# Output projection of the last two token tiles in two contraction halves, with block 4's weights loaded between them

## The reference, cut to what matters

```python
a = _rmsnorm(h, norm_mix)
proj = a @ w_in
...
h = h + jnp.concatenate([pool_out, ssd_out], axis=-1) @ w_out
h = h + _hier_moe(_rmsnorm(h, norm_ffn), router_grp_w, router_grp_b, router_exp_w, ...)
gate = jax.nn.sigmoid((_rmsnorm(h, norm_ple) @ ple_gate_w + ple_gate_b).astype(jnp.float32))
h = h + (gate * (p @ ple_proj_w).astype(jnp.float32)).astype(h.dtype)
```

## Time and profile before

| | us |
|---|---|
| median of 3 runs | 543.52 |
| the three runs | 545.23, 543.52, 539.91 |
| the profiled execution, whole | 540.01 |
| its span, first to last instruction | 538.2 |
| TensorE busy with matmuls | 503.0 (93% of the span) |
| VectorE busy | 214.2 (40%) |
| ScalarE busy | 154.3 (29%) |
| GpSimd busy | 111.6 (21%) |
| expert weights, one matrix | 1024 KB, 32 each of gate, up and down |

### The profile page before, as it was taken

One profiled execution on the slowest core, in us unless ns is written; L12 is line 12 of the kernel. 1 busy time (PEld: TensorE's weight loads), 2 busy tenths in 40 slices (PEclk: granted clock), 3 DMA queues, 4 the chain that ended last, 5 costly groups with the idle time before them and its releaser, 6 DMA issues.

```text
span 538.2 us, 7829 instructions
## 1 busy us (share of the span) xinstructions
PE 503.0 (93%) x3122; PEld 308.0 (57%) x3122; DVE 214.2 (40%) x509; ACT 154.3 (29%) x318; POOL 111.6 (21%) x169
## 2 busy tenths in 40 slices
PE   5999999999999999799999999988888989999993
PEld 4888886888545555455555555544444543444453
DVE  2187696523034556662222222212111111579344
ACT  1436263112524121112222222221121224454123
POOL 0300058994201002101111211110111112031001
PEclk9999999999999999899999999998988999999997
DMA  8993000604469905999999999999999996941012
GB/s 308 399 327 110 1 1 7 229 1 95 156 242 395 381 5 181 404 406 411 416 414 417 412 419 414 414 418 414 417 416 416 416 411 252 373 170 40 2 40 79
DMA packets 41577, 145.71 MB, mean 271 GB/s; under 512 B 14620, under 2 KB 15260, under 8 KB 32420
## 3 DMA queue, kind: packets, MB, share of 16 engines
q1 hardware_dynamic: 33956, 131.77, 62.3%
q0 software_dynamic: 5152, 8.71, 4.4%
q10 hardware_dynamic: 2432, 4.71, 2.3%
HBM read 141.24 MB, written 15.24 MB: 291 GB/s over the span
## 4 chain that ended last, share of the span: by engine, by line
PE 71%; DMA 12%; SPq 8%; DVE 6%; ACT 1%; issue 1%; POOLq 0%; ACTq 0%; POOL 0%; DVEq 0%
PE PS L1047 13%; PE PS L833 10%; PE PS L1161 10%; PE PS L639 10%; DMA mem<-in_exp_w_up 9%; PE PS L1068 7%; PE PS L610 6%; PE PS L599 5%; SPq L493 3%; SPq L497 2%; SPq L491 2%; DVE mem L1720 1%; PE PS L897 1%; DMA mem<-choice_rows 1%; DMA mem<-in_w_a 1%
## 5 line engine op out<-in xcount | busy, mean ns | idle before, releaser
L1047 PE MATMUL PS<-mem 128*64 128x256 f32 x512 | 122.1, 393 | 13.2 <-DMA mem<-in_exp_w_up 13.0
L1048 PE MATMUL PS<-mem 128*64 128x256 f32 x512 | 122.2, 394 | 0.0
L1047 PEld LDWEIGHTS PS<-mem 128*64 128x64 f32 x512 | 69.6, 141 | 49.5 <-DMA mem<-in_exp_w_up 10.6
L639 PE MATMUL PS<-mem 128*128 128x260 f32 x320 | 73.3, 386 | 0.0
L1048 PEld LDWEIGHTS PS<-mem 128*64 128x64 f32 x512 | 69.7, 141 | 0.0
L639 PEld LDWEIGHTS PS<-mem 128*128 128x128 f32 x320 | 60.0, 190 | 10.4 <-issue 1.5
L2021 DVE TENSOR_TENSOR mem<-PS,mem 64x256 f32<-64x256 f32 x32 | 13.7, 427 | 128.6 <-ACT mem L1364 128.4
L1068 PE MATMUL PS<-mem 128*64 128x512 f32 x256 | 62.0, 605 | 1.1 <-ACT mem L1370 0.7
L833 PE MATMUL PS<-mem 128*128 128x512 f32 x128 | 56.6, 596 | 0.0
L1161 PE MATMUL PS<-mem 128*128 128x512 f32 (+1 forms) x144 | 56.0, 547 | 0.0
L1364 ACT ACTIVATE mem<-PS 64x256 f32<-64x256 f32 x32 | 12.0, 375 | 113.3 <-PE PS L1048 113.3
(11 more groups left out here) (290 smaller groups left out, 550.4 us busy)
## 6 DMA issues: line engine op xcount, KB each, us to landing
mem<-in_exp_w_down SPq DMA_DIRECT2D x32, 1024.0 KB, 23.8
mem<-in_exp_w_gate SPq DMA_DIRECT2D x32, 1024.0 KB, 21.5
mem<-in_exp_w_up SPq DMA_DIRECT2D x32, 1024.0 KB, 23.5
mem<-in_w_out SPq DMA_DIRECT2D x2, 2048.0 KB, 7.3
mem<-in_ple_gate_w SPq DMA_DIRECT2D x2, 2048.0 KB, 16.6
mem<-choice_rows SPq DMA_DIRECT2D x4, 1024.0 KB, 13.4
mem<-in_x_prompt SPq DMA_DIRECT2D x4, 512.0 KB, 14.5
mem<-in_w_v SPq DMA_DIRECT2D x1, 2048.0 KB, 24.9
```

Of the source, the lines that this page charges most:

```text
L639: ins = pe.matmul(PS[b + h][:, 0:HALF], w[:, k, :], aT[:, k, h * HALF:(h + 1) * HALF], start=(k == 0), stop=(k == KT - 1))
L1047: pe.matmul(PS[0][0:S, 0:FF], rows_k, gu[slot][:, k, :], start=(k == 0), stop=(k == KT - 1))
L1048: ins = pe.matmul(PS[1][S:2 * S, 0:FF], rows_k, gu[slot][:, KT + k, :], start=(k == 0), stop=(k == KT - 1))
```

## The change

Places 3 and 4 run row groups 0 to 3 of both column halves first (`outproj_part(3, 0, 4)`, `outproj_part(4, 0, 4)`), then row groups 4 to 7. After the first half of place 4 the third count of the semaphore `s_gn_done`, now named `s_gn_part_done`, is given. SyncE waits for it and loads block 4's gate and up weights and the down weights of block 6; after all ten signals of `s_outp_done` it loads block 5's gate, up and down weights. On VectorE both residual additions of place 3 come after `place(1)`, and that of place 4's first column half after `take_h(3, 1)`.

```diff
+            sp.wait_ge(s_gn_part_done, 3)
+            load_gate_up(gu_slot(4), bass.ds(4, 1))
+            load_down(dn_slot(6), bass.ds(6, 1))
             sp.wait_ge(s_outp_done, 2 * NT)
-            for b in (4, 5):
-                load_gate_up(gu_slot(b), bass.ds(b, 1))
-            for b in (5, 6):
-                load_down(dn_slot(b), bass.ds(b, 1))
+            load_gate_up(gu_slot(5), bass.ds(5, 1))
+            load_down(dn_slot(5), bass.ds(5, 1))
...
             h_rows(1, 0)
             h_rows(1, 1)
             pe.wait_ge(s_outp_out, 4)
-            out_half(3, 0, 0, KT)
+            outproj_part(3, 0, 4)
             route(1)
             h_rows(2, 0)
             h_rows(2, 1)
             count(0)
-            out_half(3, 1, 0, KT)
+            pe.wait_ge(s_outp_out, 6)
+            outproj_part(4, 0, 4).then_inc(s_gn_part_done, 1)
             route(2)
             count(1)
-            pe.wait_ge(s_outp_out, 6)
-            out_half(4, 0, 0, KT)
+            out_half(3, 0, 4, KT)
+            out_half(3, 1, 4, KT)
+            out_half(4, 0, 4, 6)
             h_rows(3, 0)
             h_rows(3, 1)
             count(2)
-            out_half(4, 1, 0, 2)
+            out_half(4, 0, 6, KT)
             route(3)
+            out_half(4, 1, 4, 5)
             h_rows(4, 0)
             first_pair_slots()
-            out_half(4, 1, 2, 6)
+            out_half(4, 1, 5, 7)
             count(3)
-            out_half(4, 1, 6, KT)
+            out_half(4, 1, 7, KT)
...
             choose(0)
-            residual(3, 0)
             take_logits(1)
...
             place(0)
-            residual(3, 1)
             take_logits(2)
             choose(2)
             rank(1)
             place(1)
-            residual(4, 0)
+            residual(3, 0)
+            residual(3, 1)
             take_h(3, 0)
             take_h(3, 1)
+            residual(4, 0)
             rank(2)
             place(2)
             take_logits(3)
```

More of the change, by code:

```diff
@@ L419, in build @@
         s_gated = sem("s_gated")
-        s_gn_done = sem("s_gn_done")
+        s_gn_part_done = sem("s_gn_part_done")
         s_gn_ln = sem("s_gn_ln")
@@ L860, in _ @@
                                     start=True, stop=True)
-                ins.then_inc(s_gn_done, 1)
+                ins.then_inc(s_gn_part_done, 1)
             pe.wait_ge(s_inproj_out, len(COLS) - NA)
@@ L1315, in _ @@
             for g in range(2):
-                act.wait_ge(s_gn_done, g + 1)
+                act.wait_ge(s_gn_part_done, g + 1)
                 for h in range(2):
```

## The result

| | before | changed |
|---|---|---|
| median of 22 runs each, us | 542.4 | 543.89 |
| lowest and highest, us | 539.26, 545.23 | 541.98, 546.17 |
| profiled execution, us | 540.01 | 542.03 |
| its span, us | 538.2 | 540.2 |

The ratio of changed to before is 1.0047, with a 95% interval of 1.0032 to 1.0063. The change makes the kernel slower by about half a percent, 1.7 to 3.4 us. The two profiled executions differ by 2.0 us, so the pair can be used to look for the loss. A second timing of the same changed kernel, 12 runs on another chip, gave 1.0020 (0.9992 to 1.0048): smaller, and by itself not clear of no change.

The account below looks back on a forecast made before the run. The prediction took the expert weights' DMA stream, restarted when block 0 frees its buffer, as the bound. Order +1.6 us and backlog -1.6 us gave 0.0, so the median stays at 543.5 us, range 539.9 to 547.9.

Parts of the forecast that it names:

- What bounds the kernel: Expert stage: one DMA stream without a gap; the end follows its restart at block 6, when block 0 frees a buffer.
- The order's term: TensorE and VectorE before block 0: later table delays choose(3) and residual(4,1), so the buffer release moves +1.6 us, bounds 0 to 2.7.
- The backlog's term: DMA queue at block 6's gate: early loads remove transfers still queued there, -1.6 us, bounds -2.3 to -0.9.
- the smaller of the two backlogs: Queued work ahead of block 8's gate, 1.6 us (6.5 us landing against 4.9); ahead of block 6's gate it was 2.3.
- the checks on the order: Around block 0: TensorE idles 1.3 us at count(3) for VectorE; residual(4,1) and block 6's gate come 1.6 us later.
- engines idle until block 0 frees its buffer: Sign in the profile after: DMA engines idle again from about 221 us until block 0 has freed its buffer.
- gate landed in 5 to 6 us: Sign at block 6's gate transfer: it should land in about 5 us instead of 7.2.
- The sum: Whole kernel: +1.6 us of order and -1.6 us of backlog give 0.0 us against the profiled execution, 540.01 us.
- The forecast of no change within 1%: Whole kernel's time: chance 0.88 of staying within 1%, with 0.06 each for faster and slower by over 1%.
- Rival 1: DMA stream: it gains all 7.5 us of shorter queue, less 1.6 us of order, ending at 537.6 us; chance 0.05.
- Rival 2: TensorE before block 0: it is not late, so -1.6 us stands alone, 541.9 us; chance 0.22.
- Rival 3: TensorE's first select and route(4): added idle brings a second half-rate clock stretch, end +2.9 us, 546.4 us; chance 0.25.

Follow-up runs that it names:

- loads alone: Kernel before with its own matmul order, three of the six weight transfers issued about 4 us earlier; 540.81 us against 541.82, ratio 1.0002.
- Order alone: Changed kernel's order of matmuls and residual additions, all six loads put back where the kernel before has them; ratios to before 1.0028 and, run again, 1.0035.
- the repaired order: Changed kernel, early loads kept, TensorE's second half reordered and choose(3) put ahead of residual(4,0) on VectorE; 541.29 us against 541.82 before, ratio 0.9986.
- before, filled: Kernel before with two throwaway matmuls in TensorE's 1.87 us wait ahead of the second select; 540.07 us against 541.77, ratio 0.9978.
- two matmuls late: Kernel before with two throwaway matmuls on TensorE ahead of block 0, loads untouched; 543.52 us, ratio 1.0029.
- the filled version with the list late: The repaired order with first_pair_slots behind the last projection matmul and two throwaway matmuls before the second select; ratios to before 0.9965 and, again, 0.9956.

## Why the prediction was right or wrong

**What bounds the kernel: right.** The expert stage is one full DMA stream, and the end follows its restart at block 6. Fourteen profiles show it (table): difference 214.1 to 215.2 us.

**The order's term, +1.6 us: right.** Measured +1.46 at residual(4,1). The wait at count(3) was forecast as 1.3 us and is 1.24; choose(3) was forecast from 206.45 and begins at 206.66, 0.22 of which is a shift that stands in the rows already at 183.09. Nothing else that was moved costs anything visible. In block 6's gate the delay is 1.93 us: 0.22 of that shift, 1.46 of order, and 0.25 more behind it, where the second select took 3.40 us instead of 3.00.

**The backlog's term, -1.6 us: the step that failed.** The text said that the early loads take away "the smaller of the two backlogs", 1.6 us. It measures nothing: with the loads alone early the last landing does not move against the release, a release that is late by itself is not made up by any backlog, and in the changed kernel the difference to the last landing is 0.2 us longer than in before. The backlog was read from landing times (7.2 and 6.5 us against 4.9 into an idle queue) and taken for weights. The DMA queues in the trace of before, in the first microsecond after the issue of block 6's gate (226.90 to 227.95 us), and then from 227.95 to 229.5 us (queue, kind: packets, MB, share of the 16 engines):

```profile
q1 hardware_dynamic: 86, 0.29, 70.4%
q0 software_dynamic: 32, 0.13, 30.9%
...
q0 software_dynamic: 242, 0.40, 70.7%
q1 hardware_dynamic: 29, 0.20, 34.2%
```

Queue q0 is GpSimd's, q1 SyncE's. Some weights of the six were still on their way: 0.29 MB, an estimated 0.7 us at 417 GB/s. But they moved mostly in the first microsecond, when a new transfer has moved nothing yet (the changed kernel's rows below). After that the expert rows' gathers hold 71% of the engines and the weights 34%. The changed kernel in the same first microsecond (228.8 to 229.9), where nothing is left of the six:

```profile
q0 software_dynamic: 96, 0.12, 54.5%
```

No packet of weights moved here before 230.4, 1.6 us after the issue, and the engines were partly idle. So the early loads put idle engines in the place of the old weights. Order alone, with its loads late, has hardly any weights in its first microsecond either (229.96 to 231.01): 0.01 MB, 2% of the engines.

The second stretch in the changed kernel, 1.95 us later, 229.9 to 231.5:

```profile
q0 software_dynamic: 112, 0.25, 50.2%
q1 hardware_dynamic: 37, 0.30, 48.3%
```

The gathers stand beside block 6's gate here too, since they hang on the same chain of TensorE and VectorE and are as late as it is. Only a part of them found idle engines first. The gate of block 6 indeed landed sooner after its issue, 5.6 us instead of 7.2:

```profile
mem<-in_exp_w_gate SPq DMA_DIRECT2D x1, 1024.0 KB, 5.6
```

By its own landing (234.4 against 234.1) the late issue was nearly made up. But the last landing, 200 us on, is 2.12 us late. So a shorter latency of one transfer was not a gain of the stream. Order alone shows the same 5.6 us without any early load. Within 10 us of the issue, queue q1 has moved 3.46 MB in before, 0.3 MB or a little more of it old weights, and 3.26 MB in the changed kernel, all of it new. So the changed kernel is ahead by some 0.1 MB, an estimated 0.3 us of the stream at 417 GB/s, and not by 1.6. That is close to what the table shows on average (0.2 us) and less than its scatter.

Besides the checks on the order, two more of the prediction's own came out as it said (engines idle until block 0 frees its buffer, gate landed in 5 to 6 us), and both were taken as signs of a gain that they do not show. The sum was right in one term and held a second that is not there: +1.5 to +1.9 instead of 0. The forecast of no change within 1% covers the measured half a percent; the forecast of exactly none was wrong, since the interval excludes 1.

**Rival 1, all 7.5 us:** wrong, as the backlogs said and loads alone show. **Rival 2, TensorE not late:** wrong; that is what the repaired order does, and its time is that of before. **Rival 3, one more fall of the clock:** the mechanism exists, but no run shows it as a product of the change. The changed kernel's profile has one half-rate stretch there, as before has; its second profile has two, and a fall on the first select stands also in kernels with before's order (before, filled; two matmuls late): in three of five profiles with the changed order and in two of five with before's. In the timing beside its second profile the mean granted clock over the runs is 0.9833 in the changed kernel (12 runs) and 0.9831 in before (29). One microsecond at half rate is an estimated 0.0009 of that mean, so no added half-rate time shows, but some 2.4 us of it either way could hide in the scatter. Where it falls on the first select it costs that select 1.4 to 1.7 us (3.36 to 3.65 against 1.95). The clock also makes part of the spread of 5 us among runs of one kernel: over the changed kernel's 22 runs the time rises by 0.22 us for each 0.001 of mean granted clock that is missing (correlation -0.81). Where in those runs it fell is not known, since most have no profile. The Trainium skill, "TensorE: Matmul & The Clock Gate", Part 1, has activity lift the throttle; the trace agrees at the second select, where with the fillers none is slow in four profiles, against ten in ten without. The stretch in the projection of before, filled, with no idle ahead of it, shows that a wait of 1.87 us is not the only thing that such a fall can follow; its cause stays open.

## What to carry to other kernels

Where buffers limit a stream of loads, its restart is set by the engine that frees the first buffer, and loading earlier into a gap only moves the gap. A transfer's latency over the empty-queue latency is not yet a backlog that can be taken away: ask whose packets stand ahead, whether they are gone before the new transfer moves its own first packet, and whether they hang on the same chain. An edit that reorders a full engine for the sake of loads has to be costed at the other engine's serial steps, here the 2.8 us of choose(3), whose start the new order put off.

## What was not expected

Work that is thrown away made the kernel faster. Two matmuls whose result nobody reads, in a wait of 1.87 us, took the second select from 3.0 to 3.8 us down to 1.98 in all four profiles, and the kernel from 541.77 to 540.07 us, a gain that only just is clear of noise. The mean granted clock was 0.9826 over before's 35 runs there and 0.9841 over the 12 filled ones, which is within the scatter; in the filled version with the list late it was 0.9861, which is not. Together with the repaired order and first_pair_slots in a wait, the kernel is 0.35 to 0.44% under before on two chips (539.8 and 539.3 us).

The end did not feel 4 to 20 us of earlier loading beyond a few tenths, but felt each of the 6.5 us by which block 0 was put off.
